# Two RMS norms of a transformer kernel: partial sums of the squares on GpSimd ahead of TensorE

## What is computed

```python
def rms_norm(x, g):
    xf = x.astype(jnp.float32)
    y = xf * lax.rsqrt(jnp.mean(xf * xf, axis=-1, keepdims=True) + NORM_EPS)
    return (y * g.astype(jnp.float32)).astype(x.dtype)

def first_block(x, ...):
    h = rms_norm(x, pre_mix_g[l])
    z = h @ w_in[l]
    ...                                   # chunked attention and multiscale pool -> a, p
    m = jnp.concatenate([a, p], axis=-1) @ w_o[l]
    x = x + rms_norm(m, post_mix_g[l])
    h = rms_norm(x, pre_ffn_g[l])
    up = causal_dwconv(h @ w_up[l], conv_w[l], conv_b[l])
    ...                                   # gelu gate, w_down, residual; then the second block
```

## Time and profile before

| | |
|---|---|
| median of 3 runs | 2852.37 us (2852.27 to 2852.44) |
| span of the profiled execution | 2852.5 us, 0.1 above the median: nothing else lies around the span |
| TensorE (PE) busy | 2801.9 us (98%), mean granted clock 0.991 |
| VectorE (DVE) busy | 2021.8 us (71%) |
| ScalarE (ACT) busy | 1278.4 us (45%) |
| GpSimd (POOL) busy | 55.7 us (2%) |
| L1697, sums of squares | 96 records on TensorE in three norms, median 379 ns |
| L1178, VectorE's reduction of 128 x 512 | 754 ns mean |

### The profile page before, as it was taken

How to read it: one execution, slowest core, us unless ns; L and a number is a source line. 1 busy time by engine, 2 the same in 40 slices (tenths; PEclk the granted TensorE clock), 3 DMA queues, 4 the chain that set the end, 5 groups by cost and what they waited for, 6 DMA issues and landing times.

```text
span 2852.5 us, 51045 instructions
## 1 busy us (share of the span) xinstructions
PE 2801.9 (98%) x18118; PEld 2527.3 (89%) x18118; DVE 2021.8 (71%) x3153; ACT 1278.4 (45%) x1589; POOL 55.7 (2%) x60
## 2 busy tenths in 40 slices
PE   8999899999999999999999999999989999999999
PEld 8997799998899988888888998888878888888888
DVE  6766889867799987666678767878775555555554
ACT  5345455544444444212343555654444444344433
POOL 0012000000000000000002000000000000000000
PEclk9998999999999999999999999999999999999999
DMA  8883678667888885577778655666656666666665
GB/s 302 274 255 123 220 250 277 217 183 249 254 267 276 276 269 178 170 241 241 260 223 267 217 167 163 208 196 182 192 154 186 188 186 186 188 186 185 187 188 162
DMA packets 211746, 612.79 MB, mean 215 GB/s; under 512 B 23472, under 2 KB 31792, under 8 KB 210992
## 3 DMA queue, kind: packets, MB, share of 16 engines
q1 hardware_dynamic: 199296, 591.49, 66.4%
q10 hardware_dynamic: 11008, 14.60, 1.7%
q0 software_dynamic: 1328, 5.24, 0.5%
HBM read 600.75 MB, written 5.77 MB: 213 GB/s over the span
## 4 chain that ended last, share of the span: by engine, by line
PE 96%; DVE 2%; ACT 1%; issue 1%; DMA 0%; DVEq 0%; ACTq 0%
PE acc L1655 32%; PE acc L1659 26%; PE acc L1657 11%; PE acc L1658 10%; PE acc L1643 2%; PE acc L1645 2%; PE acc L1646 2%; PE acc L1653 2%; PE sums L1864 2%; PE acc L1652 1%; PE acc L1872 1%; PE turned L1857 1%; PE sums L1813 1%; PE sums L1697 1%; PE acc L1908 1%
## 5 line engine op out<-in xcount | busy, mean ns | idle before, releaser
L1021 DVE TENSOR_TENSOR wlo<-raw,whi 128x1024 fp32r<-128x1024 f32 x864 | 1059.1, 1228 | 672.1 <-ACT whi L551 670.4
L551 ACT ACTIVATE whi<-raw 128x1024 fp32r<-128x1024 f32 x864 | 914.3, 1059 | 1326.7 <-PE acc L1659 1047.4
L1659 PE MATMUL acc<-operand,wlo 128*128 128x256 f32 (+1 forms) x4752 | 1376.5, 290 | 0.0
L1659 PEld LDWEIGHTS acc<-operand,wlo 128*128 128x128 f32 x4752 | 907.2, 191 | 15.6
L1655 PE MATMUL acc<-operand,whi 128*128 128x512 f32 x2512 | 896.0, 400 | 9.6 <-DVE operand L1415 5.7
L1657 PE MATMUL acc<-operand,whi 128*128 128x256 f32 (+1 forms) x2240 | 671.3, 300 | 18.9 <-DVE wlo L1021 10.0
L1658 PE MATMUL acc<-operand,whi 128*128 128x256 f32 (+1 forms) x2240 | 669.8, 299 | 0.0
L1655 PEld LDWEIGHTS acc<-operand,whi 128*128 128x128 f32 x2512 | 473.7, 189 | 122.2 <-issue 8.8
L1655 PE MATMUL acc<-ffn_act,whi 128*128 128x512 f32 x1344 | 472.0, 395 | 0.0
L1657 PEld LDWEIGHTS acc<-operand,whi 128*128 128x128 f32 x2240 | 430.7, 192 | 32.5 <-issue 18.2
L1658 PEld LDWEIGHTS acc<-operand,whi 128*128 128x128 f32 x2240 | 430.8, 192 | 12.7
(11 more groups left out here) (229 smaller groups left out, 2081.9 us busy)
## 6 DMA issues: line engine op xcount, KB each, us to landing
cond_rows<-w_ada SPq DMA_DIRECT2D x512, 256.0 KB, 4.4
raw<-w_in SPq DMA_DIRECT2D x224, 512.0 KB, 3.6
raw<-w_up SPq DMA_DIRECT2D x176, 512.0 KB, 4.5
raw<-w_down SPq DMA_DIRECT2D x88, 512.0 KB, 3.8
raw<-w_fg SPq DMA_DIRECT2D x88, 512.0 KB, 4.0
raw<-w_fu SPq DMA_DIRECT2D x88, 512.0 KB, 4.0
raw<-w_fd SPq DMA_DIRECT2D x88, 512.0 KB, 3.7
raw<-w_o SPq DMA_DIRECT2D x32, 512.0 KB, 3.7
```

The lines of the kernel that those rows point to most:

```text
L551: act.activation(whi[j % RING][:], raw[j % RING][:], ACT.Copy).then_inc(hi_done, 1)
L1021: dve.tensor_tensor(wlo[j % RING][:], raw[j % RING][:], whi[j % RING][:].bitcast(F32), ALU.subtract).then_inc(lo_done, 1)
L1659: ins = pe.matmul(out_, l[:, x, f], mov[:, 0], start=False, stop=last)
```

## The change

In the first and second norm of the first block, GpSimd adds the four chunks of squares (four tiles each) to the first, in place, with three adds of 128 x 1024 elements, one behind the other. TensorE sums the four tiles that result. In the second norm its sums stand behind unit 6 instead of unit 5. The third norm on this path (`i == 5`, in the second block) keeps its sixteen tiles. `SQ[0]` is (0, 0) and `SQ[2]` is (4, 56): the count of squares before, and the first tile.

```diff
+        sq_added = sem("square_chunks_added")
...
         @block.gpsimd
         def _(pool):
+            def add_chunks(before, tile):
+
+                for c in range(1, 4):
+                    pool.wait_ge(sq_ready, before + c + 1)
+                    if c > 1:
+                        pool.wait_ge(sq_added, 3 * (before // 4) + c - 1)
+                    first = R[:, tile:tile + 4, :]
+                    pool.tensor_tensor(first, first, R[:, tile + 4 * c:tile + 4 * c + 4, :],
+                                       ALU.add).then_inc(sq_added, 1)
+
+            add_chunks(*SQ[0])
             pool.wait_ge(hi_done, unit(st_in, 0, 0) + 1)
...
+            add_chunks(*SQ[2])
             pool.wait_ge(hi_done, unit(st_up1a, 0, 0) + 1)
...
-                    if insert is not None and (j == 5 if st.across else gb == u == 0):
+                    if insert is not None and (j == (5 if st is st_inh else 6) if st.across else gb == u == 0):
                         sum_squares(insert)
...
-                    for kt in range(KT):
-                        pe.wait_ge(sq_ready, before + kt // 4 + 1 + (i == 5 and kt >= 14))
-                        ins = pe.matmul(NB[:, 0:S], ones, R[:, tile + kt, :], start=kt == 0, stop=kt == KT - 1)
+                    if i in (0, 2):
+                        pe.wait_ge(sq_added, 3 * (before // 4) + 3)
+                    n = KT if i == 5 else 4
+                    for kt in range(n):
+                        if i == 5:
+                            pe.wait_ge(sq_ready, before + kt // 4 + 1 + (kt >= 14))
+                        ins = pe.matmul(NB[:, 0:S], ones, R[:, tile + kt, :], start=kt == 0, stop=kt == n - 1)
```

## The result

The change makes the kernel slower: 2857.15 us (median of 11 runs, 2853.74 to 2860.18) against 2851.31 for the kernel before (11 runs, the three known ones among them, 2849.68 to 2852.78). The ratio is 1.0019 with a 95% interval of 1.0011 to 1.0028, so 5.8 us, between 3.1 and 8.0. I had forecast 2852.4, with 2849.5 to 2856.0 as the range.

A forecast was written before the change was run, and what follows sets the result against it. TensorE was taken to bound the kernel, holding 96% of the chain of waits. From 2852.5 us, minus 3.7 in norm 1 and plus 3.7 in norm 2, then 0.1 lower for the median: 2852.4, range 2849.5 to 2856.0.

The forecast's parts named there:

- Norm 1: First norm: 5.04 us of sums removed, TensorE idle 1.3 us for the adds; gain 3.7 us, ends 2.0 to 5.0.
- norm 2: Second norm: VectorE has no slack, the adds delay its operands and the next stage starts 3.7 us later.
- The exclusion: Both norms: GpSimd and VectorE hold each other up for a whole instruction when both read two SBUF tiles.
- its turns: Both norms: whichever of GpSimd and VectorE waited first goes first; adds of 2.1 us alternate with VectorE's operations.
- the late L1353: Second norm, third chunk: this VectorE operation starts 2.0 us late because the first add runs from 357.15 to 359.25.
- lo 4: Second norm, low operand of unit 4: moves from 362.15 to 365.3, so unit 4 starts 3.15 us late.
- lo 6: Second norm, low operand of unit 6: waits for the third add and ends at 376.1; unit 6 starts at 376.2.
- The rival without exclusion: Both norms: adds and VectorE don't hold each other up, 5.0 + 0.5 us gained, 2846.9; chance 6%.
- norm 2's clock: Second norm, unit 6 and sums at half clock after idling: 2 us more, 2854.4 and up to 2855.5; chance 22%.
- The base: Whole kernel: starts from the profiled span of 2852.5 us, with the runs' median 0.1 below it.
- late weights: Stage after norm 1: weights arrive late and 1 to 3 us are given back, 2853.4 to 2855.4; chance 8%.
- slow first add: First norm: GpSimd's first add is much slower than later ones, 2858.2 or an estimated 2858.4; chance 4%.

The follow-up runs named there:

- e1: The changed kernel with the adds in the first norm only, the second norm as before the change: 2850.51 against 2851.18 before, ratio 1.0001.
- e2: The changed kernel with the adds in the second norm only, its sums behind unit 6, the first norm as before: 2855.63 against 2851.18, ratio 1.0019.
- e3: The changed kernel, adds in both norms, with the second norm's sums left behind unit 5: 2853.71 against 2851.18 before, ratio 1.0007.
- e4: Kernel before plus the second norm's adds into spare tiles nobody reads; sixteen tiles summed behind unit 5: 2856.99 against 2851.18, ratio 1.0020.
- e5: e1 with GpSimd's attention pools held back until VectorE's last lo is done: 2849.77 against 2851.57 before, ratio 0.9993.
- e6: The changed kernel with matmuls on constants ahead of unit 4, unit 6 and the next stage in norm 2: 2852.59 against 2851.57 before, ratio 1.0007.
- e7: e4 with memsets of the spare tiles in place of the three adds: 2851.13 against 2851.57 before, ratio 0.9998.
- e8: e5 with the first norm's sums behind unit 6 instead of unit 5: 2847.08 against 2851.57 before, ratio 0.9983.
- e9: Kernel before with only the place changed: both norms' sixteen tiles summed behind unit 6, no adds: 2858.88 against 2851.47, ratio 1.0025.
- e12: e1 with eleven matmuls on constants in the attention: 2847.47 against 2851.47 before, ratio 0.9986.
- e10: e8 with nine matmuls on constants ahead of the attention's first transposes and two ahead of the second: 2845.49 against 2851.47 before, ratio 0.9975.
- e11: The kernel before with eleven matmuls on constants in the attention: 2848.67 against 2851.47, ratio 0.9989.

## Why the prediction was wrong

Terms of the sum from the traces, against what the medians say (us against before, unless named). "Norm 1" is the time from unit 5's last matmul to the second score, less 176.87; "order" the 1.35 of the overtaken lo, put in where the trace shows it overtaken; "norm 2" what the next stage starts later from unit 0, with the low clock behind it.

| kernel | norm 1 | order | norm 2 | sum | medians |
|---|---|---|---|---|---|
| after | -2.09 | +1.35 | +5.63 +1.5 | +6.4 | +5.8 |
| e1 | -2.39 | +1.35 | 0 | -1.0 | -0.7 |
| e2 | 0 | 0 | +4.17 | +4.2 | +4.5 |
| e3 | -2.69 | +1.35 | +1.99 | +0.7 | +2.5 |
| e4 | 0 | 0 | +5.79 | +5.8 | +5.8 |
| e5 | -1.16 | 0 | 0 | -1.2 | -1.8 |
| e6 | -2.68 | +1.35 | +4.13 | +2.8 | +1.0 |
| e7 | 0 | 0 | 0 | 0 | -0.4 |
| e8 | -4.64 | 0 | 0 | -4.6 | -4.5 |
| e9 | +0.55 | 0 | +6.16 +1.4 | +8.1 | +7.4 |

Each sum is within 2.0 us of its medians; the runs of one kernel span 2 to 7 us, and a sum stands on one execution. The clock's share in the attention is in no column.

- **Mechanism: right.** The exclusion, its turns, the late L1353, lo 4 and lo 6 came where they were put: from unit 0 unit 4 starts at 18.18 us (forecast 18.0), unit 6 at 28.01 (27.6). The rival without exclusion is out (L1366's 3.24 us, and e4).
- **The step that failed: norm 2's clock.** I had priced unit 6 and the sums at full speed and kept the low clock as a rival of 22% with some 2 us. It fell in unit 6 (1.48 us). My argument against it, that slow units 4 and 5 would shorten the wait before unit 6, held only in part: they ran at 0.57 for a while, the wait was 2.38 instead of 3.75, and the clock fell again all the same. A second fall, behind the 3.19 us before the next stage, cost 1.5 more; no case of mine held it, although the idle stretch followed from my own numbers (unit 7 done at 383.7, the next stage at 387.05). Norm 2 lost 7.1 instead of 3.7. Where the clock fell neither in unit 6 nor behind the next stage's start, the forecast was near: the loss was 4.17 in e2 and 4.13 in e6. From the sums' end to the next stage the forecast held (6.3 us, measured 6.27).
- **Norm 1: sized too well.** 3.7 forecast, 2.1 measured. The turns took 8.93 us from the first add's start to the third's end (21.85 to 30.78) instead of 8.6, since an add needs 2.25 to 2.38 us rather than 2.1. The estimate that I had made from the Trainium skill (GPSIMD Engine Reference, "Performance versus the Vector engine"), 2.25, agrees better than my row. The larger part is where the engines stood: the first add began 0.5 us later than I had put it, and TensorE began unit 5's last matmul 0.8 us earlier than in before's execution (27.80 and 28.57), so less of the adds was hidden. With the sums behind unit 5 the gain was 2.1, 2.4, 2.7, 2.7 and 3.3 us in the executions of after, e1, e3, e6 and e12; I had taken one execution's distances as fixed.
- **What no case had: the order in the attention.** I had said that a shift at the first norm is carried on unchanged. It isn't where two engines' requests lie 0.05 us apart; 1.35 of norm 1's gain went there.
- **The base.** I took the profiled span as representative and the device time as 0.1 below it. It was 1.8 above, on a late execution, so something does lie around the span. The two partly cancel, by luck: the later runs put before at 2851.3 instead of 2852.4.
- The other rivals: no late weights (the stage after norm 1 runs at full clock, busy throughout), and no slow first add.
- **The range** was too narrow at the top: it held the clock in unit 6 but not both falls together with a smaller gain in norm 1.

The change joins two things with opposite values. In the first norm, where VectorE runs ahead, the adds are worth 4.5 us once their wait is covered and GpSimd's pools are held back (e8). In the second, where VectorE feeds TensorE just in time, the adds start unit 4 3.3 us late, and the new place uncovers the wait for lo 6. e10 beats both kernels: 2845.49, some 6 us below before.

## What to carry to other kernels

Before moving an add to GpSimd, look whether VectorE has slack at that moment: where it makes operands just in time, each add held it up for as long as the add still ran (3.24 us instead of 1.23 for one operation here), and TensorE with it. Work that TensorE does between two units also covers the waits that lie there, so moving it has a price of its own (e9). And an added idle stretch of TensorE is to be priced twice: its length, and, where the clock falls, the matmuls behind it at half clock (about 1.5 us each time here).

## What the runs showed of the hardware that I had not expected

- The clock falls behind quite short waits, but not each time: after 1.45 us before unit 6 in e2 and 2.12 before the next stage in e3 it stayed at 1.00, after 2.38 in the changed kernel and 2.48 in e9 it fell. The length alone doesn't settle it: behind the same 3.19 us before the next stage it fell in the changed kernel and in e9, and stayed at 1.00 in e2. The Trainium skill (TensorE: Matmul & The Clock Gate, "Part 1: The HAM clock gate") says that the clock follows how busy the array has been lately, and that the moment of its change differs from run to run. The traces agree, with attentions of 38.2 and 40.0 us in kernels that do the same work there. Useless matmuls kept it up in all three gaps of e6 and in the first of e11, where eleven of them are worth 2.8 us.
- The first add on GpSimd asks 0.24 us after the copy before it where GpSimd has added nothing yet (205.52 to 205.76 in before, the same in e7 and e9), and 0.15 us where the norm's adds ran earlier (202.11 to 202.26 in e1). These 0.09 us decide who goes first, VectorE or GpSimd. That an earlier use is the reason fits all these traces, but wasn't tried by itself.
- The first add itself costs nothing extra: in the changed kernel it asks at 21.61, VectorE's lo holds until 21.85 (20.62 + 1.23), and it is done at 24.12, so 2.27 us, like the later ones.
